# The depthwise convolution of a two-block transformer kernel: from VectorE and GpSimd to VectorE alone

## The chip, the cores and the metric

The kernel runs on one core of a Trainium2 chip. The metric is the device time of one execution in microseconds (us), as the median over several runs. The engines are named as in the profile: PE is TensorE (PEld its weight loads), DVE is VectorE, ACT is ScalarE, POOL is GpSimd, and SP issues the weight stream's DMAs.

## What is computed

The reference runs two transformer blocks on 256 tokens of width 2048, in fp32. In the first block, the input projection feeds three mixers: a gated linear recurrence (sections a_f, a_q, a_i, a_g), a dilated attention (b_q, b_k, b_v) and a convolution module. The change touches only that module:

```python
def conv_module(a, gate, conv_w, conv_b, ln_g, ln_b):
    u = a * jax.nn.sigmoid(gate)
    y = lax.conv_general_dilated(u, conv_w[:, None, :], window_strides=(1,),
                                 padding=((C_KERNEL - 1, 0),),
                                 dimension_numbers=('NWC', 'WIO', 'NWC'),
                                 feature_group_count=C_WIDTH) + conv_b
    return jax.nn.silu(layer_norm(y, ln_g, ln_b))
```

It has 768 channels and 31 taps. Channels lie on partitions, so the module has 6 tiles of 128 channels x 256 tokens, and one tap of one tile is one multiply-add of 128x256 elements: 6 x 31 = 186 steps, each adding to what the step before left in the same tile.

## The kernel before

Every matrix product is made from fp32 weights split in two parts. The weights come as a stream of 1 MB blocks through four buffers (`raw`), in an order that is written out by hand (`SECTIONS`). For each block b, ScalarE makes the high part (`split_high`, line 530), DVE makes the low part as the difference (`split_low`, line 1685), and PE multiplies: first the high part with both parts of the activations (32 matmuls, line 1020, "high pass"), then the low part (16 matmuls, line 1029, "low pass"). There are two pairs of part buffers. ScalarE may start block b+2 once PE has begun the low pass of block b, DVE may start its split of b+2 once block b is done, and a `raw` buffer is free for the next load once DVE's split has read it. Each engine works through its own instruction list in order.

Around the change the order is:

- The start section makes the modulated activations and the two branches of the convolution module, and DVE multiplies them into `upad` (line 1792), six tiles with 30 zero columns ahead of each.
- The 16 blocks of a_f and a_q follow, one product each. DVE runs a loop of 16 rounds over them: one `split_low` and six steps of the convolution on tiles 0 to 2 (lines 1804 and 1807), three chains side by side, 93 steps in all.
- GpSimd does tiles 3 to 5 meanwhile (lines 460 and 465). It has no multiply-add here, so for each tap it scales the three tiles into a scratch tile `ctap` and adds them to `cy`: 93 scalings of 256 columns and 30 adds of 768 columns.
- DVE then scales `fP` and `kk`, 16 instructions (lines 1817 and 1818).
- The level stage runs over 43 blocks (a_i, b_v, b_k, b_q, a_g, and nine of gate). PE, ScalarE and DVE each go block by block; from the fifth block on each block has one of 36 "levels" of the recurrence beside it: DVE prepares operands (lines 1838 and 1839), advances two running products (lines 1846 and 1848), PE makes 8 small products (line 1207), DVE reads them (line 1867). The first 14 blocks (a_i and b_v) go in pairs: PE runs the high pass of two blocks (64 matmuls), then the low pass of both (32), and DVE makes both splits together. The four blocks before level 0 are the lead (`LAG`).
- At level 19 PE waits for the whole convolution and sums it for the layer norm.

The wait for GpSimd's steps is `pe.wait_ge(conv_side, CONV_SIDE)`, the one for DVE's is `pe.wait_ge(conv_tap, CONV_DVE * C_TAPS)`. A step waits on DVE's own counter `conv_tap` until the step before it in its chain has been written.

Of the kernel before, what the change touches and what calls it, by code (L numbers as in the profile page):

```python
# [7 lines left out]
ALU = mybir.AluOpType  # L8
# [6 lines left out]
S = 256  # L15
# [6 lines left out]
A_HEADS, B_HEADS, B_SLOTS = 8, 12, 4  # L22
C_TILES, C_TAPS = 6, 31
EARLY = 2
CONV_DVE = 3
CONV_SIDE = (C_TILES - CONV_DVE) * C_TAPS + C_TAPS - 1
FF1, FF2 = 8192 // P, 5632 // P
QUARTER = 4
UP2 = FF2 // QUARTER
# [122 lines left out]
def two_blocks_kernel(nc, stream, x_t, ctx_t, vec_d, const_d, lvl_mask_d, ident_d, rel_bias, c_rows, scratch, x_keep, out_t):  # L152
    with ExitStack() as ctx:
# [3 lines left out]
        def sem(name):  # L157
            return ctx.enter_context(nc.semaphore(name))
# [47 lines left out]
        def v(name, i=0, n=1):  # L206
            return vec[:, VEC[name] + i:VEC[name] + i + n]
# [18 lines left out]
        bv = region(33024, 2, 768)  # L226
        squares = region(18432, 6, S)
        upad = region(19968, 6, 30 + S)
        ctap = region(18432, 3, S)
        cg = region(22016, 6, S)  # L230
        cy = yc = region(28672, 6, S)
        yb = region(30208, 2, S)
# [88 lines left out]
        sq_part, x_ready, hf_part, hh_part, h_part = (sem(n) for n in ("sq_part", "x_ready", "hf_part", "hh_part", "h_part"))  # L321
        dve_step, act_step = sem("dve_step"), sem("act_step")
        brow_mm, brow_ready, brow_out, bias_in = sem("brow_mm"), sem("brow_ready"), sem("brow_out"), sem("bias_in")
        conv_tap, conv_side, mean_mm, conv_cent, yc_in, conv_done = (
            sem(n) for n in ("conv_tap", "conv_side", "mean_mm", "conv_cent", "yc_in", "conv_done"))
        lvl_prep, lvl_mm, lvl_read, o_mm, o_copied, ya_ready = (
            sem(n) for n in ("lvl_prep", "lvl_mm", "lvl_read", "o_mm", "o_copied", "ya_ready"))
        qk_mm, log_ready, exp_ready, dg_ready = sem("qk_mm"), sem("log_ready"), sem("exp_ready"), sem("dg_ready")
# [46 lines left out]
        def conv_tap_of(t, tap):  # L375

            return v("conv_w", t * C_TAPS + tap)
# [63 lines left out]
        @block.gpsimd  # L441
        def _(pool):
            pool.memset(eps, EPS).then_inc(eps_set, 1)
            pool.memset(cpad, 0.0).then_inc(fills, 1)
            pool.memset(ones[:, :], 1.0).then_inc(fills, 1)
            pool.memset(head_sum[:, :], 0.0).then_inc(fills, 1)
            pool.wait_ge(fills, 3)
            pool.memset(head_sum[:, 7:8], 1.0).then_inc(fills, 1)

            pool.wait_ge(brow_ready, 1)  # L450
            pool.memset(upad[:, :, 0:30], 0.0).then_inc(pads_set, 1)
            pool.wait_ge(pads_set, 1)
            pool.wait_ge(ca_read, 2)
            n = 0
            for tap in range(C_TAPS):
                if tap:
                    pool.wait_ge(conv_side, n)
                for t in range(CONV_DVE, C_TILES):
                    dst = ctap[:, t - CONV_DVE, :] if tap else cy[:, t, :]
                    pool.tensor_scalar(dst, upad[:, t, tap:tap + S], conv_tap_of(t, tap), None if tap else v("conv_b", t),  # L460
                                       ALU.mult, *(() if tap else (ALU.add,))).then_inc(conv_side, 1)
                    n += 1
                if tap:
                    pool.wait_ge(conv_side, n)
                    pool.tensor_tensor(cy[:, CONV_DVE:, :], cy[:, CONV_DVE:, :], ctap, ALU.add).then_inc(conv_side, 1)
                    n += 1
            assert n == CONV_SIDE


        @block.scalar  # L470
# [527 lines left out]
        def _(pe):  # L998
# [231 lines left out]
            for n in range(BESIDE_LEVELS):  # L1230
                s = n - LAG
                part, i = LATE[n]
                if part in ("a_i", "b_v"):
                    if i % 2 == 0:
                        rest = gemm_tokens(gb(part, i), opH, 2, later=True)
                    else:
                        rest()
                else:
                    gemm_T(gb(part, i), opH)
                if s % 9 == 0 and 0 < s <= 36:  # L1240
                    outputs(s // 9 - 1)
                if s == 19:

                    pe.wait_ge(conv_tap, CONV_DVE * C_TAPS)
                    pe.wait_ge(conv_side, CONV_SIDE)
                    for t in range(C_TILES):
                        ins = pe.matmul(M[2][:, S:512], ones[:, :], cy[:, t, :], start=(t == 0), stop=(t == C_TILES - 1))
                    ins.then_inc(mean_mm, 1)
                if s == 22:
                    norm(squares, C_TILES)  # L1250
                if 0 <= s < 36:
                    level(s)
                if s in (36, 37):
                    for h in range(6) if s == 36 else range(6, 8):
                        pe.wait_ge(o_sq, h // 2 + 1)
                        ins = pe.matmul(M[0][0:8, 0:S], head_sum[:, 7 - h:15 - h], fP[:, h, :], start=(h == 0), stop=(h == 7))
                    if s == 37:
                        norms[0] += 1
                        ins.then_inc(ms_ready, 1)
# [385 lines left out]
        def _(dve):  # L1645
# [147 lines left out]
                ins.then_inc(ca_read, 1)  # L1793
            split_low(KT + 1)

            taps = 0
            for i in range(16):
                split_low(gb("a_f") + i + 2)
                if i == 0:
                    dve.wait_ge(ca_read, 3)  # L1800
                for _ in range(min(6, C_TAPS * CONV_DVE - taps)):
                    t, j = taps % CONV_DVE, taps // CONV_DVE
                    if j == 0:
                        ins = dve.tensor_scalar(cy[:, t, :], upad[:, t, 0:S], conv_tap_of(t, 0), v("conv_b", t), ALU.mult, ALU.add)
                    else:
                        dve.wait_ge(conv_tap, taps - CONV_DVE + 1)
                        ins = dve.scalar_tensor_tensor(cy[:, t, :], upad[:, t, j:j + S], conv_tap_of(t, j), cy[:, t, :],  # L1807
                                                       ALU.mult, ALU.add)
                    ins.then_inc(conv_tap, 1)
                    taps += 1  # L1810
            assert taps == C_TAPS * CONV_DVE

            for i in range(8):
                was_read(dve, gb("a_f", i))
# [10 lines left out]

            for n in range(LAG):
                split_late(n)

            for s in range(36):
                quarter, L = s // 9, s % 9  # L1830
                hs = slice(2 * quarter, 2 * quarter + 2)
                f_, q_, k_ = fP[:, hs, :], qq[:, hs, :], kk[:, hs, :]
                if L == 0:
                    dve.memset(suf, 1.0).then_inc(lvl_prep, 1)
                    dve.wait_ge(lvl_prep, s + 1)
                else:
                    dve.wait_ge(lvl_mm, s)
                    dve.tensor_tensor(qs, q_, f_, ALU.mult)
                    dve.tensor_tensor(ks, k_, suf, ALU.mult).then_inc(lvl_prep, 1)
                    dve.wait_ge(lvl_prep, s + 1)  # L1840
                    if L < 8:
                        w = 1 << (L - 1)
                        fv_ = f_.rearrange("p h (b two w) -> p (h b) two w", two=2, w=w)
                        sv_ = suf.rearrange("p h (b two w) -> p (h b) two w", two=2, w=w)
                        nb = 2 * S // (2 * w)
                        step(dve.tensor_tensor(sv_[:, :, 0, :], sv_[:, :, 0, :],
                                               fv_[:, :, 1, w - 1:w].to_broadcast([P, nb, w]), ALU.mult))
                        step(dve.tensor_tensor(fv_[:, :, 1, :], fv_[:, :, 1, :],
                                               fv_[:, :, 0, w - 1:w].to_broadcast([P, nb, w]), ALU.mult))

                if s == 20:
                    dve.wait_ge(mean_mm, 1)
                    step(dve.tensor_scalar(rstd[:, S:512], M[2][:, S:512], 1.0 / (C_TILES * P), None, ALU.mult))
                    dve.tensor_tensor(cy, cy, over_tiles(rstd[:, S:512], C_TILES), ALU.subtract).then_inc(conv_cent, 1)
                if s == 23:
                    inverted()
                    dve.wait_ge(conv_cent, 1)
                    dve.tensor_tensor(cy, cy, over_tiles(rstd[:, 0:S], C_TILES), ALU.mult).then_inc(yc_in, 1)
                split_late(s + LAG)
                dve.wait_ge(lvl_mm, s + 1)  # L1860
                if s % 9 == 0 and s:
                    dve.wait_ge(o_mm, quarter)
                bank4 = M[s % 2][:, :].rearrange("p (a b) -> p a b", a=4)
                if L == 0:
                    last = dve.tensor_tensor(attn, bank4, over_tiles(ident[:, :], 4), ALU.mult)
                elif L < 8:
                    last = dve.copy_predicated(attn, lvl_mask[:, L:L + 1, :].to_broadcast([P, 4, P]), bank4)
                else:
                    last = dve.tensor_copy(attx, bank4[:, 0:2, :])
                last.then_inc(lvl_read, 1)  # L1870
                dve.wait_ge(lvl_read, s + 1)

            split_late(36 + LAG)
            split_late(37 + LAG)
            inverted()
# [531 lines left out]
```

## Time and profile before

| | |
|---|---|
| median of 3 runs | 3377.06 us (3375.75 to 3380.68) |
| the profiled execution | 3368.44 us, its span 3366.6 us |
| PE, DVE, ACT, POOL busy | 96%, 68%, 40%, 6% of the span |
| mean granted PE clock | 0.98 of 2.4 GHz |
| a_f and a_q blocks | about 155 to 254 us |
| level stage: paired blocks, then single ones | about 254 to 356 us, then to about 560 us |

The profiled execution is 8.6 us under the median of the runs. Times in the trace count from the start of the span. A timeline row gives its start, its length, the engine, the line, the operation, output and inputs, the number of instructions merged in it, and in brackets how long the engine sat idle before it and what ended that.

### The profile page before, as it was taken

What the parts mean: (1) busy time and instruction counts of PE and PEld (TensorE: products, weight loads), DVE (VectorE), ACT (ScalarE), POOL (GpSimd) and SP (SyncE); (2) the same over time, 40 slices, a digit from 0 to 9 for tenths busy, and PEclk for the clock granted to TensorE, in tenths of its full rate; (3) what the DMA queues carried; (4) which work ended last, traced back from release to release, by engine and by line L of the source; (5) the groups of instructions that cost most, each with busy time, mean ns of one, the idle gap of its engine ahead of it and who ended that gap; (6) DMA issues with size and microseconds to landing.
All of it is one profiled execution on the core that took longest, in us unless ns stands there. A gap on an engine that the chain in (4) does not pass through costs nothing.

```text
span 3366.6 us, 59486 instructions
## 1 busy us (share of the span) xinstructions
PE 3236.8 (96%) x26148; PEld 3131.8 (93%) x26148; DVE 2279.4 (68%) x2532; ACT 1332.6 (40%) x1455; POOL 214.6 (6%) x133
## 2 busy tenths in 40 slices
PE   7898999899998999999999999999998999999998
PEld 6898999799998999999998899989888999999998
DVE  2498765578877778888956756644566666666664
ACT  2332344433434433333355233421355444343444
POOL 0199400000000000000000000000000000000000
PEclk9999999999999999999999999999999999999999
DMA  9854434388885687767744754354333575655643
GB/s 349 328 183 153 171 139 146 113 306 331 321 313 192 247 325 257 272 240 286 287 168 154 287 222 185 121 208 159 117 126 124 176 251 184 217 214 188 238 168 120
DMA packets 106430, 722.87 MB, mean 215 GB/s; under 512 B 11676, under 2 KB 15388, under 8 KB 27196
## 3 DMA queue, kind: packets, MB, share of 16 engines
q1 hardware_dynamic: 100368, 703.64, 56.9%
q10 hardware_dynamic: 5804, 15.43, 1.5%
q8 instruction: 207, 3.39, 0.4%
q14 instruction: 51, 0.42, 0.0%
HBM read 712.40 MB, written 6.55 MB: 214 GB/s over the span
## 4 chain that ended last, share of the span: by engine, by line
PE 88%; DVE 7%; DMA 2%; ACT 1%; issue 1%; ACTq 0%; DVEq 0%
PE gemm L1020 49%; PE gemm L1029 25%; DVE sb_arena L1807 2%; DVE sb_parts L1685 2%; PE mix L1108 2%; DMA sb_raw<-stream 2%; PE mix L1020 1%; PE gemm L1143 1%; PE mix L1207 1%; PE mix L1468 1%; DMA sb_arena<-x_t 1%; ACT sb_parts L530 1%; DVE sb_arena L1731 1%; PE mix L1029 1%; PE gemm L1537 1%
## 5 line engine op out<-in xcount | busy, mean ns | idle before, releaser
L530 ACT ACTIVATE sb_parts<-sb_raw 128x2048 fp32r<-128x2048 f32 (+2 forms) x499 | 913.6, 1833 | 1683.4 <-PE gemm L1029 1387.0
L1685 DVE TENSOR_TENSOR sb_parts<-sb_raw,sb_parts 128x2048 fp32r<-128x2048 f32 (+2 forms) x499 | 1096.3, 2198 | 400.1 <-ACT sb_parts L530 220.3
L1020 PE MATMUL gemm<-op_h,sb_parts 128*128 128x256 f32 x7232 | 899.3, 283 | 0.5 <-DVE sb_arena L1792 0.5
L1020 PEld LDWEIGHTS gemm<-op_h,sb_parts 128*128 128x128 f32 x7232 | 875.6, 189 | 1.5 <-issue 0.9
L1029 PE MATMUL gemm<-op_h,sb_parts 128*128 128x256 f32 x3616 | 466.8, 282 | 5.9 <-DVE sb_parts L1685 5.9
L1029 PEld LDWEIGHTS gemm<-op_h,sb_parts 128*128 128x128 f32 x3616 | 444.8, 188 | 7.3 <-DVE sb_parts L1685 7.3
L1020 PE MATMUL gemm<-op_up,sb_parts 128*128 128x256 f32 x3456 | 438.7, 284 | 11.4 <-DVE op_up L2246 11.4
L1020 PEld LDWEIGHTS gemm<-op_up,sb_parts 128*128 128x128 f32 x3456 | 422.8, 189 | 13.7 <-DVE op_up L2246 12.2
L1029 PE MATMUL gemm<-op_up,sb_parts 128*128 128x256 f32 x1728 | 228.2, 284 | 0.0
L1666 DVE CUSTOM_DVE_ANT_0 sb_raw<-sb_raw,sb_arena,sb_vec 128x2048 f32<-128x2048 f32 x96 | 224.3, 2348 | 1.1
L1029 PEld LDWEIGHTS gemm<-op_up,sb_parts 128*128 128x128 f32 x1728 | 216.2, 190 | 0.0
L1020 PE MATMUL gemm<-op_hw,sb_parts 128*128 128x512 f32 (+1 forms) x992 | 185.0, 344 | 0.0
L1020 PEld LDWEIGHTS gemm<-op_hw,sb_parts 128*128 128x128 f32 x992 | 156.8, 189 | 23.6
L1658 DVE CUSTOM_DVE_ANT_0 sb_raw<-sb_raw,sb_arena,sb_vec 128x2048 f32<-128x2048 f32 x64 | 149.8, 2346 | 0.0
L2237 DVE SCALAR_TENSOR_TENSOR sb_arena<-gemm,sb_vec,sb_arena 128x255 f32<-128x255 f32 x88 | 42.5, 483 | 150.0 <-ACT sb_arena L971 150.0
L460 POOL TENSOR_SCALAR sb_arena<-sb_arena,sb_vec 128x256 f32<-128x256 f32 x93 | 127.6, 1385 | 114.2 <-DVE sb_arena L1792 111.3
L1020 PE MATMUL gemm<-sb_parts,op_hw 128*128 128x256 f32 x1024 | 125.7, 286 | 0.9 <-ACT sb_parts L530 0.9
L1020 PEld LDWEIGHTS gemm<-sb_parts,op_hw 128*128 128x128 f32 x1024 | 124.3, 191 | 2.1 <-ACT sb_parts L530 1.1
L1974 DVE TENSOR_TENSOR sb_arena<-gemm,sb_arena 128x256 f32<-128x256 f32 x80 | 33.9, 424 | 102.8 <-PE gemm L1029 102.8
L1029 PE MATMUL gemm<-op_hw,sb_parts 128*128 128x512 f32 (+1 forms) x496 | 94.9, 344 | 0.0
L1108 PE MATMUL mix<-sb_arena,sb_ones 128*128 128x256 f32 x256 | 74.0, 419 | 19.1 <-ACT sb_arena L498 19.1
L1029 PEld LDWEIGHTS gemm<-op_hw,sb_parts 128*128 128x128 f32 x496 | 78.9, 189 | 11.9
(341 smaller groups left out, 3483.7 us busy)
## 6 DMA issues: line engine op xcount, KB each, us to landing
sb_raw<-stream SPq DMA_DIRECT2D x611, 1024.0 KB, 5.0
sb_raw<-stream SPq DMA_DIRECT2D x64, 704.0 KB, 4.1
sb_raw<-stream SPq DMA_DIRECT2D x16, 768.0 KB, 7.8
sb_arena<-c_rows ACTq DMA_DIRECT2D x3, 1024.0 KB, 8.1
bias_rows<-sb_arena ACTq DMA_DIRECT2D x1, 2304.0 KB
sb_arena<-x_t ACTq DMA_DIRECT2D x4, 512.0 KB, 17.9
sb_arena<-ctx_t SPq DMA_DIRECT2D x1, 2048.0 KB, 10.8
x_keep<-sb_arena ACTq DMA_DIRECT2D x1, 2048.0 KB, 6.3
```

Source lines behind the costliest of these rows:

```text
L460: pool.tensor_scalar(dst, upad[:, t, tap:tap + S], conv_tap_of(t, tap), None if tap else v("conv_b", t), ALU.mult, *(() if tap else (ALU.a ...
L530: act.activation(parts[:, b % 2, 0, 0:kt, :], raw[:, slot, 0:kt, :], ACT.Copy).then_inc(hi_ready, 1)
L1020: ins = pe.matmul(out, l, r, start=(opens and i == 0 and x is xh), stop=False, skip_group_check=True)
L1029: ins = pe.matmul(out, l, r, start=False, stop=(i == len(terms) - 1), skip_group_check=True)
L1108: ins = pe.matmul(M[1][:, 0:S], ones[:, :], src[:, k, :], start=(k == 0), stop=(k == KT - 1))
L1143: ins = pe.matmul(out[:, i * S:(i + 1) * S], w, opH[:, p, k, :], start=(k == i == part == p == 0), stop=(k == KT - 1 and part == 1), skip_ ...
L1658: dve.tensor_tensor_reduce(w, w, c1_row, 1.0, v("b_ada", a), ALU.mult, ALU.add, mod1[:, a:a + 1])\
L1666: dve.tensor_tensor_reduce(w, w, c2_row, 1.0, v("b_mod", a), ALU.mult, ALU.add, mod2[:, 0, a:a + 1])\
L1685: dve.tensor_tensor(parts[:, b % 2, 1, 0:kt, :], raw[:, slot, 0:kt, :], parts[:, b % 2, 0, 0:kt, :].bitcast(F32), ALU.subtract).then_inc(t ...
L1807: ins = dve.scalar_tensor_tensor(cy[:, t, :], upad[:, t, j:j + S], conv_tap_of(t, j), cy[:, t, :], ALU.mult, ALU.add)
L1974: dve.tensor_tensor(t, bank(b0 + j)[:, 0:S], t, ALU.add).then_inc(bank_read[BANK[b0 + j]], 1)
L2237: step(dve.scalar_tensor_tensor(y[:, 1:S], src[:, 0:S - 1], w0, y[:, 1:S], ALU.mult, ALU.add))
```

## The change

All 186 steps run on DVE, in six chains, one for each tile, tap after tap. They are spread: eight steps after each of the 16 splits of the a_f and a_q loop (128), five after each of the four lead steps (20), three in each level until none is left (38, levels 0 to 12). GpSimd keeps only the memset of the padding columns; `ctap` and `conv_side` go. DVE's wait on its own counter `ca_read` moves ahead of the first split of the loop. PE's wait at level 19 is for the one counter.

```diff
-CONV_DVE = 3
-CONV_SIDE = (C_TILES - CONV_DVE) * C_TAPS + C_TAPS - 1
+CONV_STEPS = C_TILES * C_TAPS
...
             pool.memset(upad[:, :, 0:30], 0.0).then_inc(pads_set, 1)
-            pool.wait_ge(pads_set, 1)
-            pool.wait_ge(ca_read, 2)
-            n = 0
-            for tap in range(C_TAPS):
-                if tap:
-                    pool.wait_ge(conv_side, n)
-                for t in range(CONV_DVE, C_TILES):
-                    dst = ctap[:, t - CONV_DVE, :] if tap else cy[:, t, :]
-                    pool.tensor_scalar(dst, upad[:, t, tap:tap + S], conv_tap_of(t, tap), None if tap else v("conv_b", t),
-                                       ALU.mult, *(() if tap else (ALU.add,))).then_inc(conv_side, 1)
-                    n += 1
-                if tap:
-                    pool.wait_ge(conv_side, n)
-                    pool.tensor_tensor(cy[:, CONV_DVE:, :], cy[:, CONV_DVE:, :], ctap, ALU.add).then_inc(conv_side, 1)
-                    n += 1
...
-                    pe.wait_ge(conv_tap, CONV_DVE * C_TAPS)
-                    pe.wait_ge(conv_side, CONV_SIDE)
+                    pe.wait_ge(conv_tap, CONV_STEPS)
...
-            taps = 0
-            for i in range(16):
-                split_low(gb("a_f") + i + 2)
-                if i == 0:
-                    dve.wait_ge(ca_read, 3)
-                for _ in range(min(6, C_TAPS * CONV_DVE - taps)):
-                    t, j = taps % CONV_DVE, taps // CONV_DVE
+            taps = [0]
+
+            def conv_taps(n):
+                for _ in range(min(n, CONV_STEPS - taps[0])):
+                    j, t = divmod(taps[0], C_TILES)
                     if j == 0:
                         ins = dve.tensor_scalar(cy[:, t, :], upad[:, t, 0:S], conv_tap_of(t, 0), v("conv_b", t), ALU.mult, ALU.add)
                     else:
-                        dve.wait_ge(conv_tap, taps - CONV_DVE + 1)
+                        dve.wait_ge(conv_tap, taps[0] - C_TILES + 1)
                         ins = dve.scalar_tensor_tensor(cy[:, t, :], upad[:, t, j:j + S], conv_tap_of(t, j), cy[:, t, :],
                                                        ALU.mult, ALU.add)
                     ins.then_inc(conv_tap, 1)
-                    taps += 1
-            assert taps == C_TAPS * CONV_DVE
+                    taps[0] += 1
+
+            dve.wait_ge(ca_read, 3)
+            for i in range(16):
+                split_low(gb("a_f") + i + 2)
+                conv_taps(8)
...
             for n in range(LAG):
                 split_late(n)
+                conv_taps(5)
...
                 split_late(s + LAG)
+                conv_taps(3)
                 dve.wait_ge(lvl_mm, s + 1)
```

## Rows read from the trace of the kernel before

**Rows 1.** The page, part 1: busy time, share of the span and instructions.

```profile
PE 3236.8 (96%) x26148; PEld 3131.8 (93%) x26148; DVE 2279.4 (68%) x2532; ACT 1332.6 (40%) x1455; POOL 214.6 (6%) x133
```

**Rows 2.** Busy time of each engine by stretch, with the mean granted clock.

```profile
core 0: us, PE busy (x) PEld busy (x) DVE busy (x) ACT busy (x) POOL busy (x), PEclk, DMA share, GB/s
...
265.60:288.40 22.80, 18.39 (x128) 18.24 (x129) 17.38 (x21) 8.03 (x5) 22.16 (x16) 0.85 0.38 139
288.40:356.40 68.00, 67.54 (x571) 67.10 (x570) 60.30 (x52) 22.29 (x18) 66.37 (x36) 1.00 0.42 156
```

**Rows 3.** Timeline of PE, the a_f and a_q blocks (matmuls only).

```profile
160.75 3.96 PE L1020 MATMUL gemm<-op_h,sb_parts 128*128 128x256 f32 x32
164.55 2.06 PE L1029 MATMUL gemm<-op_h,sb_parts 128*128 128x256 f32 x16
166.45 3.96 PE L1020 MATMUL gemm<-op_h,sb_parts 128*128 128x256 f32 x32
...
217.76 2.16 PE L1029 MATMUL gemm<-op_h,sb_parts 128*128 128x256 f32 x16 [0.86 <-DVE sb_parts L1685]
```

**Rows 4.** Timeline of PE, the first pairs of the level stage.

```profile
254.59 7.83 PE L1020 MATMUL gemm<-sb_parts,op_h 128*128 128x256 f32 x64 [0.49 <-ACT sb_parts L530]
265.69 5.55 PE L1029 MATMUL gemm<-sb_parts,op_h 128*128 128x256 f32 x32 [3.27 <-DVE sb_parts L1685]
271.07 7.76 PE L1020 MATMUL gemm<-sb_parts,op_h 128*128 128x256 f32 x64
283.16 5.47 PE L1029 MATMUL gemm<-sb_parts,op_h 128*128 128x256 f32 x32 [4.32 <-DVE sb_parts L1685]
288.46 7.75 PE L1020 MATMUL gemm<-sb_parts,op_h 128*128 128x256 f32 x64
296.06 1.05 PE L1207 MATMUL mix<-sb_arena 128*128 128x128 f32 x8
296.86 4.04 PE L1029 MATMUL gemm<-sb_parts,op_h 128*128 128x256 f32 x32
```

**Rows 5.** Timeline of DVE, one round of the a_f loop.

```profile
174.43 2.28 DVE L1685 TENSOR_TENSOR sb_parts<-sb_raw,sb_parts 128x2048 fp32r<-128x2048 f32 x1
176.63 4.71 DVE L1807 SCALAR_TENSOR_TENSOR sb_arena<-sb_arena,sb_vec 128x256 f32<-128x256 f32 x6
181.27 2.28 DVE L1685 TENSOR_TENSOR sb_parts<-sb_raw,sb_parts 128x2048 fp32r<-128x2048 f32 x1
```

**Rows 6.** Line 1807 (chained steps): ns min/median/max, first and last start.

```profile
L1807 DVE SCALAR_TENSOR_TENSOR sb_arena<-sb_arena,sb_vec x90: 470/694/2070, 166.3 to 268.1; 128x256 f32<-128x256 f32 x90
```

**Rows 7.** Timeline of POOL beside that round.

```profile
171.67 3.01 POOL L460 TENSOR_SCALAR sb_arena<-sb_arena,sb_vec 128x256 f32<-128x256 f32 x3
174.77 3.65 POOL L465 TENSOR_TENSOR sb_arena<-sb_arena 128x768 f32<-128x768 f32 x1
```

**Rows 8.** Lines 1817 and 1818 (16 scales): ns min/median/max, first and last start.

```profile
L1817 DVE TENSOR_SCALAR sb_arena<-sb_arena,sb_small x8: 480/558/1999, 268.4 to 277.4; 128x256 f32<-128x256 f32 x8
...
L1818 DVE TENSOR_SCALAR sb_arena<-sb_arena,sb_small x8: 348/530/531, 268.9 to 277.8; 128x256 f32<-128x256 f32 x8
```

**Rows 9.** Timeline of DVE in a later stage, GpSimd idle.

```profile
2573.40 0.48 DVE L1731 SCALAR_TENSOR_TENSOR sb_arena<-sb_arena,sb_small,sb_rstd 128x256 f32<-128x256 f32 x1
2573.79 0.48 DVE L1737 SCALAR_TENSOR_TENSOR op_h<-sb_arena,sb_mod,op_h 128x256 fp32r<-128x256 f32 x1
```

**Rows 10.** Timeline of DVE, one level of the single-block stage, GpSimd idle.

```profile
384.61 0.73 DVE L1867 COPY_PREDICATED sb_arena<-sb_lvl_mask,mix 128x512 f32<-128x512 uint8 x1
385.38 0.69 DVE L1838 TENSOR_TENSOR sb_arena<-sb_arena 128x512 f32<-128x512 f32 x1
...
386.71 0.43 DVE L1846 TENSOR_TENSOR sb_arena<-sb_arena 128x256 f32<-128x256 f32 x1
...
389.00 2.29 DVE L1685 TENSOR_TENSOR sb_parts<-sb_raw,sb_parts 128x2048 fp32r<-128x2048 f32 x1 [1.40 <-ACT sb_parts L530]
```

**Rows 11.** Timeline of ACT: the load that came late.

```profile
191.60 1.92 ACT L530 ACTIVATE sb_parts<-sb_raw 128x2048 fp32r<-128x2048 f32 x1 [7.13 <-DMA sb_raw<-stream]
```

More of the change, by code:

```diff
@@ L228, in two_blocks_kernel @@
         upad = region(19968, 6, 30 + S)
-        ctap = region(18432, 3, S)
         cg = region(22016, 6, S)
@@ L323, in two_blocks_kernel @@
         brow_mm, brow_ready, brow_out, bias_in = sem("brow_mm"), sem("brow_ready"), sem("brow_out"), sem("bias_in")
-        conv_tap, conv_side, mean_mm, conv_cent, yc_in, conv_done = (
-            sem(n) for n in ("conv_tap", "conv_side", "mean_mm", "conv_cent", "yc_in", "conv_done"))
+        conv_tap, mean_mm, conv_cent, yc_in, conv_done = (
+            sem(n) for n in ("conv_tap", "mean_mm", "conv_cent", "yc_in", "conv_done"))
         lvl_prep, lvl_mm, lvl_read, o_mm, o_copied, ya_ready = (
@@ L451, in _ @@
             pool.memset(upad[:, :, 0:30], 0.0).then_inc(pads_set, 1)
-            pool.wait_ge(pads_set, 1)
-            pool.wait_ge(ca_read, 2)
-            n = 0
-            for tap in range(C_TAPS):
-                if tap:
-                    pool.wait_ge(conv_side, n)
-                for t in range(CONV_DVE, C_TILES):
-                    dst = ctap[:, t - CONV_DVE, :] if tap else cy[:, t, :]
-                    pool.tensor_scalar(dst, upad[:, t, tap:tap + S], conv_tap_of(t, tap), None if tap else v("conv_b", t),
-                                       ALU.mult, *(() if tap else (ALU.add,))).then_inc(conv_side, 1)
-                    n += 1
-                if tap:
-                    pool.wait_ge(conv_side, n)
-                    pool.tensor_tensor(cy[:, CONV_DVE:, :], cy[:, CONV_DVE:, :], ctap, ALU.add).then_inc(conv_side, 1)
-                    n += 1
-            assert n == CONV_SIDE
         @block.scalar
@@ L1871, in _ @@
                 dve.wait_ge(lvl_read, s + 1)
+            assert taps[0] == CONV_STEPS
             split_late(36 + LAG)
```

## The prediction

> **What bounds the kernel now.** I read the page first. PE is busy 96% of the span [rows 1]. So the engine that loses the conv (GpSimd, 6%) and the one that takes it over (DVE, 68%) matter only where PE waits for DVE. The busy shares by stretch then say where that is [rows 2]: from 265.6 to 288.4 us PE works 18.39 of 22.80 us at a mean granted clock of 0.85, and from 288.4 to 356.4 us 67.54 of 68.00 at 1.00.
>
> PE's own timeline gives the size. A block of the a_f and a_q sections takes 166.45 - 160.75 = 5.70 us when nothing is late, 1.90 of it the low pass [rows 3]. DVE's round beside it, one low split and six taps, takes 181.27 - 174.43 = 6.84 us [rows 5]. At first PE lives on a lead, because DVE's split is due only 3.8 us into a block; once the lead is used up each low pass waits for DVE, 0.86 us in the row at 217.76 us [rows 3], seven such rows in all. After block 16 the waits go on: 3.27 us before the low pass of the first pair and 4.32 us before that of the second [rows 4]. After each of these two the low pass of 32 matmuls takes 5.38 and 5.30 us instead of 3.80 (2 x 1.90), and the mean granted clock of that stretch is 0.85, so part of it ran at 1.2 instead of 2.4 GHz.
>
> **Why DVE's round is that long.** The split takes 176.63 - 174.43 = 2.20 us, six taps 4.64 us, 0.773 each [rows 5]. The 90 taps range from 0.47 to 2.07 us with a median of 0.69 [rows 6], for one and the same size. In each round GpSimd runs three scalings and an add of 768 columns; the add at 174.77 us takes 3.65 us and so ends some 1.8 us into DVE's taps [rows 7]. The 16 scales that DVE does next, also beside GpSimd, show the same spread, 0.35 to 2.00 us [rows 8]. With GpSimd idle, the same instruction on the same size (SCALAR_TENSOR_TENSOR, 256 columns, all in SBUF) starts every 0.39 to 0.40 us (2573.40 and 2573.79, and 20 more such rows up to 2581.71, 0.396 on the mean) [rows 9]. I take 0.396 us for a tap after the change.
>
> The Trainium skill (SBUF — State Buffer, "SBUF: two separate sides") says that a DVE operation with two SBUF inputs and a GpSimd operation that reads SBUF hold a shared port pair exclusively, and the loser blocks for the whole instruction. The add row agrees; beside the scalings of about 1.0 us [rows 7] the median tap is only about 0.2 us longer than the shortest, which is less than that rule would give. With GpSimd idle both come to the same.
>
> **The change, part by part.**
>
> 1. *GpSimd's 93 scalings and 30 adds go.* They are not on the chain (their result is waited for at level 19, about 420 us; they end at 373 us). What they cost is DVE's delay, counted below.
>
> 2. *Eight taps a round instead of six, 16 rounds.* DVE: 2.20 + 8 x 0.396 = 5.37 us, under PE's 5.70. So PE sets the pace. From 160.75 us, where block 2 starts, 15 blocks end at 160.75 + 15 x 5.70 = 246.2 us; before, they ended at 254.59 - 0.49 = 254.1 us [rows 3, 4]. Gain 7.9 us. DVE's round is then held by ScalarE's high part, which ends about 0.2 us after the block, and its last round ends at 246.4 + 5.4 = 251.8 us. The wait for `ca_read` now stands ahead of the first split; it is DVE's own earlier instruction, nothing but that split is behind it, I bound it by 0 and the 2.2 us of a split, and take 0: it is hidden by ScalarE's high part.
>
> 3. *The 16 scales behind the stage* took 9.9 us beside GpSimd. They are not edited, but the two slowest lose 1.5 us each. I take 0.48 us each, 7.6 us, though 0.35 may do [rows 8]: DVE is at 259.4 us.
>
> 4. *Five taps after each of the four lead steps* add 2.0 us each. PE: first pair high pass from 246.7 us (0.49 behind ScalarE, as before), low from 254.3; its split is ready at 248.6. No wait, 3.27 + 1.58 us gone. Low ends at 258.1. DVE: five taps to 261.4, two splits (2 x 2.20) to 265.8. PE: high pass of the second pair 258.5 (again behind ScalarE, which the stall hid before: minus 0.47) to 266.1, then low. The split is 0.3 us early: 4.32 + 1.50 us gone. Low ends at 269.9. DVE: ten taps to 269.8, splits from 270.2 to 274.6, five taps and the memset to 277.2. PE's third pair: high pass 270.4 (minus 0.30) to 278.0, and level 0 finds its operands ready. Gain of this stretch 3.27 + 1.58 + 4.32 + 1.50 - 0.77 = 9.9 us.
>
> 5. *Three taps in each of levels 0 to 12* (38 in all: 186 - 128 - 20) add 1.2 us each. A level costs DVE 389.00 - 384.61 - 1.40 = 3.0 us [rows 10]. In the pair stage, two levels: 2 x 3.0 + 2 x 2.2 + 6 x 0.396 = 12.8 us against PE's 11.4 + 2 x 0.80 = 13.0 [rows 4]. The order inside matters more: from the end of a low pass DVE does two splits, three taps, the bank read (0.77) and the next operands (1.33) [rows 10], ready about 8.0 us later with the 0.3 us that ScalarE takes; PE wants them after a level and a high pass, 0.8 + 7.6 = 8.4 us. Now, beside GpSimd, PE is idle only some 0.5 us of this stage (68.00 - 67.54, [rows 2]); I let that go too. In the single-block stage DVE idles 1.40 us a level [rows 10]; three taps leave 0.2.
>
> 6. *From level 13 on* the instruction streams are the same, and the conv is finished (level 12) well ahead of its use at level 19. What is due after is relative to PE, so the gain is kept.
>
> Sum: 7.9 + 9.9 + 0.5 = 18.3 us. The profiled execution took 3368.44 us (span 3366.6 and 1.84 around it); after, 3350.1. The median of the runs shown is 8.6 us above that execution, so I put the change on it: 3377.06 - 18.3 = 3358.8, say 3359 us. Bounds: PE's waits and slow matmuls between 206 and 356 us, with the 0.77 us that stay, are 7.9 + 10.7 + 0.5 = 19 us, so the gain ends near there, 21 with what I don't see. From the other side a tap costs 0.48 if nothing overlaps, 0.773 if GpSimd was never the cause.
>
> **Rivals.**
>
> A. *Taps don't overlap: 0.48 us each, the record's own length [rows 9].* Then a round is 2.28 + 8 x 0.48 = 6.12 us, over 5.70. PE's lead covers all 16 rounds, but DVE leaves the stage at 259.1 us, has the scales and five taps done at 269.2, the two splits at 273.8, where PE wanted them at 267.2: 6.6 us and 1.5 of low clock; 1 us before the first pair. Gain 18.3 - 9.1 = 9 us, 3368. Against it: starts 0.396 apart [rows 9]. The Trainium skill (VectorE: DVE Perf Modes, "The DRAIN you can't avoid") would have it so: the next operation does not start until the pipe is empty. The trace's overlapping records speak against that here. The same outcome, a gain of 7 to 14 us, comes if the thin margins of parts 4 and 5 (0.3 and 0.4 us) are missed, each miss costing itself and up to 1.5 us of clock. Chance of both together 0.17.
>
> B. *Slower: the tap's price is its own, not GpSimd's.* If a tap stays at 0.773, a round is 8.4 us: the last ends near 294 us, against 268.4 now, 26 us later; ten of the extra taps before the levels add 8 us, the pair stage 5 x (4.6 - 0.7) = 20 us, three single levels 2 us: 56 us, 3433. Where it turns: at 0.58 a round is as long as now (2.2 + 8 x 0.58 = 6.84), and the taps between stage and levels and those in the pair stage make it some 7 us slower; at 0.50 the same count leaves a gain of 7; so about 0.54. For it: the taps now cost 0.77 on the mean. Against it: the same instruction in [rows 9], and the 0.47 of the shortest taps [rows 6]. Chance 0.05, all prices above 0.54 together.
>
> C. *No change: PE goes faster but the weights don't come.* At 191.60 us ScalarE waited 7.13 us for a load [rows 11], while the stage's one store was still going out. If the stream held PE at its old pace, nothing would be won: 3377. Against it: PE took its blocks at the full 5.70 us up to about 206 us, this late load among them, and the stream kept up. A late load more likely costs 1 to 3 us. Chance of within 0.2%: 0.07.
>
> D. *More than 22 us*, by something that I don't see: 0.03.
>
> **How the numbers follow.** The forecast (3355 to 3362) has 0.68, A 0.17, B 0.05, C 0.07, D 0.03. 0.2% is 6.8 us, about what a measurement of this kernel tells from no change. A still counts as faster: 0.68 + 0.17 + 0.03 = 0.88. The range takes in A: 3353 to 3369.
>
> **What would show it.** Right: PE's blocks start 5.70 us apart up to about 246 us and the second pair's low pass starts without a wait; the 180 chained taps last 0.47 to 0.48 us each, none 2 us; DVE's split has a short idle before it, put down to ScalarE, in each round; the 1.2 GHz stretches at 265.9 and 282.9 us are gone; from level 13 the trace is the old one, 18 us earlier. Wrong: taps over 0.5 us, a PE wait on the DVE split behind the 16 scales, levels whose operands PE waits for.

## The result, and the profile after

The changed kernel took 3360.18 us (median of 5 runs, 3347.63 to 3365.33) against 3379.46 us for the kernel before (5 runs, 3375.75 to 3382.06): a ratio of 0.9948, 95% interval 0.993 to 0.9966. Faster by 19.3 us; 18.3 were forecast, 3359 us as the time.

PE's timeline answers [rows 3] and [rows 4]. The blocks come every 166.68 - 160.98 = 5.70 us, up to the last; of the two long waits nothing is left, and 0.4 to 0.5 us of waiting for ScalarE stand ahead of each of the first three pairs:

```profile
160.98 3.96 PE L1002 MATMUL gemm<-op_h,sb_parts 128*128 128x256 f32 x32
...
166.68 3.96 PE L1002 MATMUL gemm<-op_h,sb_parts 128*128 128x256 f32 x32
...
247.07 7.83 PE L1002 MATMUL gemm<-sb_parts,op_h 128*128 128x256 f32 x64 [0.49 <-ACT sb_parts L512]
254.74 3.96 PE L1011 MATMUL gemm<-sb_parts,op_h 128*128 128x256 f32 x32
259.10 7.84 PE L1002 MATMUL gemm<-sb_parts,op_h 128*128 128x256 f32 x64 [0.40 <-ACT sb_parts L512]
266.77 3.95 PE L1011 MATMUL gemm<-sb_parts,op_h 128*128 128x256 f32 x32
271.12 7.83 PE L1002 MATMUL gemm<-sb_parts,op_h 128*128 128x256 f32 x64 [0.40 <-ACT sb_parts L512]
278.79 1.06 PE L1189 MATMUL mix<-sb_arena 128*128 128x128 f32 x8
```

DVE's timeline answers [rows 5] and [rows 8]. Eight steps take 3.25 us, 0.40 each, and the split that follows has waited 0.24 us for ScalarE. The 16 scales, now lines 1802 and 1803, start 0.29 us apart on the mean:

```profile
172.81 2.29 DVE L1666 TENSOR_TENSOR sb_parts<-sb_raw,sb_parts 128x2048 fp32r<-128x2048 f32 x1 [0.23 <-ACT sb_parts L512]
175.01 3.25 DVE L1788 SCALAR_TENSOR_TENSOR sb_arena<-sb_arena,sb_vec 128x256 f32<-128x256 f32 x8
178.50 2.29 DVE L1666 TENSOR_TENSOR sb_parts<-sb_raw,sb_parts 128x2048 fp32r<-128x2048 f32 x1 [0.24 <-ACT sb_parts L512]
...
252.23 0.41 DVE L1802 TENSOR_SCALAR sb_arena<-sb_arena,sb_small 128x256 f32<-128x256 f32 x1
252.55 0.35 DVE L1803 TENSOR_SCALAR sb_arena<-sb_arena,sb_small 128x256 f32<-128x256 f32 x1
252.81 0.41 DVE L1802 TENSOR_SCALAR sb_arena<-sb_arena,sb_small 128x256 f32<-128x256 f32 x1
...
257.04 2.07 DVE L1788 SCALAR_TENSOR_TENSOR sb_arena<-sb_arena,sb_vec 128x256 f32<-128x256 f32 x5
259.03 4.49 DVE L1666 TENSOR_TENSOR sb_parts<-sb_raw,sb_parts 128x2048 fp32r<-128x2048 f32 x2
```

The 180 chained steps all last the same (ns min/median/max; [rows 6] had 470/694/2070):

```profile
L1788 DVE SCALAR_TENSOR_TENSOR sb_arena<-sb_arena,sb_vec x180: 470/478/486, 165.6 to 360.9; 128x256 f32<-128x256 f32 x180
```

The busy shares of the stretch that was at a mean clock of 0.85 in [rows 2] (PE, PEld, DVE, ACT, POOL, then the clock): PE works 22.40 of 22.80 us, all at 2.4 GHz.

```profile
265.60:288.40 22.80, 22.40 (x190) 22.23 (x189) 17.53 (x24) 8.47 (x6) 0.00 (x0) 1.00 0.39 148
```

A measure that leaves out what happens elsewhere is the distance from PE's first a_f block to the first single block of the level stage (block 14), read from PE's timeline. It is 356.36 - 154.97 = 201.4 us before and 338.23 - 155.21 = 183.0 us after: 18.4 us less.

But the two profiled spans differ by 8.3 us only (3366.6 and 3358.3). DVE's splits, numbered from 0 at the start of the kernel, show where the rest went. Number 150 starts 18.9 us earlier than before (1056.7 against 1075.6 us), number 270 only 11.9 (1756.9 against 1768.8), number 300 only 9.4. Between 1100 and 1650 us PE is busy all the time at a granted clock of 1.00; it simply does fewer matmuls in the same 550 us. Of before, then of after:

```profile
core 0: us, PE busy (x), PEclk, DMA share, GB/s
1100.00:1650.00 550.00, 550.00 (x4637) 1.00 0.75 272
```

```profile
core 0: us, PE busy (x), PEclk, DMA share, GB/s
1100.00:1650.00 550.00, 550.00 (x4586) 1.00 0.75 272
```

That is 118.6 ns from matmul to matmul before and 119.9 after. This distance is called the pitch below, and a part of a trace at 119.9 a slow stretch. Whether it came with the change had to be tested.

### The profile page after: what moved, and what is told of

The parts are those of the page before. It is cut to its first block, busy times and chain, and to the rows that moved or that the text cites. A ratio compares the mean times of both kernels' runs of the same rounds, so it can differ in the third digit from the quotient of the medians.

```text
span 3358.3 us, 59453 instructions
## 1 busy us (share of the span) xinstructions
PE 3243.2 (97%) x26148; PEld 3137.8 (93%) x26148; DVE 2261.3 (67%) x2625; ACT 1332.7 (40%) x1455; POOL 1.7 (0%) x10
## 4 chain that ended last, share of the span: by engine, by line
PE 92%; DVE 4%; DMA 2%; ACT 1%; issue 1%; ACTq 0%; DVEq 0%
PE gemm L1002 51%; PE gemm L1011 25%; PE mix L1090 2%; DMA sb_raw<-stream 2%; PE mix L1002 1%; PE gemm L1125 1%; PE mix L1189 1%; PE mix L1449 1%; ACT sb_parts L512 1%; DMA sb_arena<-x_t 1%; DVE sb_parts L1666 1%; DVE sb_arena L1712 1%; PE mix L1011 1%; PE gemm L1518 1%; PE gemm L1525 1%
## 5 line engine op out<-in xcount | busy, mean ns | idle before, releaser
L1975 DVE TENSOR_TENSOR sb_arena<-sb_arena 128x256 f32<-128x256 f32 x64 | 27.1, 424 | 75.1 <-ACT sb_arena L756 73.6
```

## The experiments

In the table, "between" is the distance from the first a_f block to block 14 in the one profiled execution of each kernel. The second trace of the kernel before comes from a single execution of 3381.74 us. Ratios are against the kernel before, run on the same chip in the same job.

| kernel | median us | ratio, 95% interval | between, us |
|---|---|---|---|
| before (first trace; again) | 3379.46 | 1 | 201.4; 201.5 |
| changed | 3360.18 | 0.9948 (0.993 to 0.9966) | 183.0 |
| changed, again | 3356.11 | 0.9946 (0.9925 to 0.9966) | 183.1 |
| changed, third | 3353.70 | 0.9939 (0.992 to 0.9958) | 183.1 |
| before, GpSimd's half left out | 3358.81 | 0.9944 (0.9922 to 0.9965) | 182.9 |
| changed, one chain | 3367.21 | 0.9967 (0.9953 to 0.9981) | 190.3 |
| changed, GpSimd beside | 3408.85 | 1.0095 (1.0067 to 1.0124) | 236.6 |
| changed, GpSimd scalings only | 3365.12 | 0.997 (0.9957 to 0.9983) | 192.9 |
| changed, GpSimd adds only | 3394.05 | 1.0049 (1.0031 to 1.0066) | 221.3 |
| changed, twelve a round | 3370.09 | 0.9982 (0.9969 to 0.9994) | 197.1 |
| changed, split ahead of the norm | 3351.62 | 0.9924 (0.9906 to 0.9942) | 183.1 |
| the same, again | 3351.89 | 0.9936 (0.9917 to 0.9956) | 183.2 |

**The changed kernel again**, with no edit.

> The changed kernel again, nothing altered. In its first trace the block after the single-block boundary (block 14 of the level stage) starts 18.1 us earlier than before, but PE's matmuls of the up and down stretches (1114 to 1672 us) follow one another by 120.0 ns where the kernel before had 118.6, which gives some 9 us back. Theory P (the two pitches are a state that an execution falls into): the part up to 338 us repeats within 0.5 us (block 14 starts at 338), while the stretches at 120 ns lie elsewhere or are gone, and the end moves with them, by up to 10 us. Rival Q (the slower pitch comes with the change): the same stretches at 120 ns again, and the same end.

The distance repeated within 0.1 us and the slow stretch was gone; the span was 3348.7 us, 9.6 less than in the first trace of the same kernel, some 7 of them by the pitch:

```profile
core 0: us, PE busy (x), PEclk, DMA share, GB/s
1100.00:1650.00 550.00, 550.00 (x4637) 1.00 0.75 276
```

**GpSimd's half left out of the kernel before.** DVE's part is as it was: three chains, six steps a round.

```diff
-CONV_SIDE = (C_TILES - CONV_DVE) * C_TAPS + C_TAPS - 1
+CONV_SIDE = 1
...
-            for tap in range(C_TAPS):
...
+            pool.memset(cy[:, CONV_DVE:, :], 0.0).then_inc(conv_side, 1)
```

> The kernel before, with GpSimd's half of the convolution left out: tiles 3 to 5 are set to zero by one memset, DVE still does its 93 steps, six a round. Theory (GpSimd's SBUF traffic lengthens DVE's steps): a step follows the next by 0.396 us instead of 0.773, DVE's round is 2.2 + 6 x 0.396 = 4.6 us, PE sets the pace with 5.70, no wait before the low passes of the first two pairs, block 14 of the level stage starts at 338 us as in the changed kernel (356.4 before), the end about 18 us under the kernel before. Rival (a step costs 0.77 by itself, or the gain comes from six chains instead of three): the round stays at 6.8 us and the time within 2 us of the kernel before.

The same six steps as in [rows 5] take 2.46 us instead of 4.71, DVE is idle 1.03 us a round, and PE waits for it nowhere. The distance is 182.9 us. So the whole gain of 18.4 us had been the price of GpSimd's work beside DVE, and nothing of them is due to six chains or to the spreading, which only keep the price of the added steps at nothing. (This kernel computes only three of the six tiles; it measures time alone.)

```profile
174.79 2.46 DVE L1794 SCALAR_TENSOR_TENSOR sb_arena<-sb_arena,sb_vec 128x256 f32<-128x256 f32 x6
178.28 2.29 DVE L1672 TENSOR_TENSOR sb_parts<-sb_raw,sb_parts 128x2048 fp32r<-128x2048 f32 x1 [1.03 <-ACT sb_parts L517]
```

**One chain.** Tile after tile, each step waiting for the one ahead.

```diff
-                    j, t = divmod(taps[0], C_TILES)
+                    t, j = divmod(taps[0], C_TAPS)
...
-                        dve.wait_ge(conv_tap, taps[0] - C_TILES + 1)
+                        dve.wait_ge(conv_tap, taps[0])
```

> The changed kernel, but the 186 steps run tile after tile, so that each waits for the one ahead of it to be written. Theory (six chains let the steps overlap; a dependent DVE operation starts about 0.03 us after the end of the one ahead, so 0.51 us apart): round 2.2 + 8 x 0.51 = 6.3 us, over 5.70, DVE leaves the a_q stage near 262 us instead of 252, PE waits some 3 us before the low pass of the first pair and some 3 us before that of the second, with low-clock stretches behind; block 14 starts near 347 instead of 338, the time 7 to 11 us over the changed kernel. Rival (the waits are free, the order doesn't matter): same as the changed kernel within 2 us.

Eight dependent steps take 176.18 - 172.13 = 4.05 us, 0.506 each, as expected, and PE waits 1.98 us before the low pass of the first pair and 3.58 us before that of the second. The distance grows by 7.2 us, the median by 11 us over the changed kernel run beside it.

```profile
172.13 4.13 DVE L1788 SCALAR_TENSOR_TENSOR sb_arena<-sb_arena,sb_vec 128x256 f32<-128x256 f32 x8
176.18 2.28 DVE L1666 TENSOR_TENSOR sb_parts<-sb_raw,sb_parts 128x2048 fp32r<-128x2048 f32 x1
```

```profile
259.18 4.04 PE L1011 MATMUL gemm<-sb_parts,op_h 128*128 128x256 f32 x32 [1.98 <-DVE sb_parts L1666]
...
275.09 5.19 PE L1011 MATMUL gemm<-sb_parts,op_h 128*128 128x256 f32 x29 [3.58 <-DVE sb_parts L1666]
```

**GpSimd beside.** The changed kernel with GpSimd's old loop kept, its sums going to a scratch tile.

```diff
+                    dst = ctap[:, t - CONV_DVE, :] if tap else cside[:, t - CONV_DVE, :]
...
+                    pool.tensor_tensor(cside, cside, ctap, ALU.add).then_inc(conv_side, 1)
```

> The changed kernel, with GpSimd also doing its old 93 scalings and 30 adds, into scratch that nobody reads; PE waits for them at level 19 as before. Theory (contention): a step costs 0.77 us again, the round is about 8.4 us, block 14 starts near 410 us, and the time is 40 to 75 us over the changed kernel and well over the kernel before. Rival (GpSimd beside DVE costs little when DVE has six chains): within 10 us of the changed kernel.

The median is 53 us over the changed kernel and 31 over the kernel before, so the sign of the change hangs on GpSimd being idle. A round takes 183.47 - 175.61 = 7.86 us, some longer, less than the 8.4 expected; block 14 starts at 389 us, not 410.

```profile
175.61 2.28 DVE L1687 TENSOR_TENSOR sb_parts<-sb_raw,sb_parts 128x2048 fp32r<-128x2048 f32 x1
177.81 5.73 DVE L1809 SCALAR_TENSOR_TENSOR sb_arena<-sb_arena,sb_vec 128x256 f32<-128x256 f32 x8
183.47 2.28 DVE L1687 TENSOR_TENSOR sb_parts<-sb_raw,sb_parts 128x2048 fp32r<-128x2048 f32 x1
```

**Which of GpSimd's instructions.** The same kernel with the 93 scalings alone, and with the 30 adds alone. The main lines left out are shown; the scalings then follow one another without a wait, and so do the adds, which in the full loop lie some 7 us apart.

```diff
-                    pool.wait_ge(conv_side, n)
-                    pool.tensor_tensor(cside, cside, ctap, ALU.add).then_inc(conv_side, 1)
```

```diff
-                    pool.tensor_scalar(dst, upad[:, t, tap:tap + S], conv_tap_of(t, tap), None if tap else v("conv_b", t),
-                                       ALU.mult, *(() if tap else (ALU.add,))).then_inc(conv_side, 1)
```

> The changed kernel with GpSimd beside it doing 93 scalings of 256 columns into a scratch tile, and no adds. Theory (a scaling lengthens a DVE step by some 0.2 us every other time, the add by 1.6): steps 0.5 us apart on the mean, round about 6.3 us, the time 6 to 12 us over the changed kernel. Rival (a GpSimd instruction of any kind keeps a two-input DVE operation out for its whole length): steps at least 1 us apart while GpSimd runs, 40 us or more over the changed kernel.

> The changed kernel with GpSimd beside it doing 30 adds of 768 columns in scratch, and no scalings. Theory: each add (1.83 us, two inputs in SBUF) keeps one DVE step waiting for about 1.6 us, 30 x 1.6 = 48 us of DVE time at the start of the a_f stage; with PE's lead of 6 us and a few us of DVE idle taken off, 30 to 42 us over the changed kernel. Rival (the scalings are what costs, being three times as many): under 15 us over the changed kernel.

Beside the scalings, eight steps take 179.04 - 175.06 = 3.98 us, 0.50 each, the longest 0.70 us; the distance grows by 9.8 us. Beside the adds the steps are 1.96 us apart (15.68 for eight) and even the split takes 3.88 instead of 2.28; GpSimd's 30 adds (ns min/median/max) run one behind the other until 222 us, and one DVE step gets in between two of them. The distance grows by 38.2 us. Apart the two cost 48.0 us of distance, together (the kernel with both) 53.5, and the adds have most of it in both counts. How the 18.4 us of the kernel before divide between them was not measured. DVE timeline of the first kernel with its chained steps and GpSimd's scalings (ns min/median/max), then of the second (with the six unchained first steps, one input each, ahead), and GpSimd's line in the second:

```profile
175.06 4.06 DVE L1804 SCALAR_TENSOR_TENSOR sb_arena<-sb_arena,sb_vec 128x256 f32<-128x256 f32 x8
179.04 2.28 DVE L1682 TENSOR_TENSOR sb_parts<-sb_raw,sb_parts 128x2048 fp32r<-128x2048 f32 x1
```

```profile
L1804 DVE SCALAR_TENSOR_TENSOR sb_arena<-sb_arena,sb_vec x180: 469/479/704, 165.7 to 369.9; 128x256 f32<-128x256 f32 x180
```

```profile
L461 POOL TENSOR_SCALAR sb_arena<-sb_arena,sb_vec x93: 922/1035/4846, 154.2 to 288.3; 128x256 f32<-128x256 f32 x93
```

```profile
162.38 11.54 DVE L1800 TENSOR_SCALAR sb_arena<-sb_arena,sb_vec 128x256 f32<-128x256 f32 x6
...
181.61 15.75 DVE L1803 SCALAR_TENSOR_TENSOR sb_arena<-sb_arena,sb_vec 128x256 f32<-128x256 f32 x8
197.29 3.88 DVE L1681 TENSOR_TENSOR sb_parts<-sb_raw,sb_parts 128x2048 fp32r<-128x2048 f32 x1
```

```profile
L461 POOL TENSOR_TENSOR sb_arena<-sb_arena x30: 1812/1862/3775, 154.6 to 218.6; 128x768 f32<-128x768 f32 x30
```

**Twelve steps a round**, not spread.

```diff
-                conv_taps(8)
+                conv_taps(12)
```

> The changed kernel with the steps not spread: twelve after each split of the a_f and a_q loop, so all but six are done in it and none is left for the levels. Theory (DVE's round against PE's 5.70 decides): round 2.2 + 12 x 0.396 = 6.95 us, PE's lead of some 6 us lasts five or six rounds, then PE goes at DVE's pace, and the low pass of the first pair waits until about 268 us (254.7 in the changed kernel); block 14 starts at 351 to 354 us instead of 338, the time is 13 to 15 us over the changed kernel, only some 4 us under the kernel before. Rival (only the total of DVE's work counts, not where it lies): same as the changed kernel within 3 us.

DVE's round is 216.86 - 209.91 = 6.95 us. From 212 us on PE waits 0.9 to 1.0 us in each block, and 3.52 before the first pair's low pass, which starts at 267.99 us, at 268 as expected. 14.1 us of the 18.4 are gone: with the steps placed so, the removal of GpSimd's work would have bought 4.3 us of distance. The median is 7.1 us under the kernel before (3377.23 us in that job), where some 4 were expected.

```profile
209.91 2.29 DVE L1666 TENSOR_TENSOR sb_parts<-sb_raw,sb_parts 128x2048 fp32r<-128x2048 f32 x1
212.11 4.84 DVE L1788 SCALAR_TENSOR_TENSOR sb_arena<-sb_arena,sb_vec 128x256 f32<-128x256 f32 x12
216.86 2.29 DVE L1666 TENSOR_TENSOR sb_parts<-sb_raw,sb_parts 128x2048 fp32r<-128x2048 f32 x1
```

```profile
267.99 5.56 PE L1011 MATMUL gemm<-sb_parts,op_h 128*128 128x256 f32 x32 [3.52 <-DVE sb_parts L1666]
```

**One edit more: the low split ahead of the norm at level 23.**

```diff
-                if s == 23:
-                    inverted()
-                    dve.wait_ge(conv_cent, 1)
-                    dve.tensor_tensor(cy, cy, over_tiles(rstd[:, 0:S], C_TILES), ALU.mult).then_inc(yc_in, 1)
                 split_late(s + LAG)
                 conv_taps(3)
+                if s == 23:
+                    inverted()
+                    dve.wait_ge(conv_cent, 1)
+                    dve.tensor_tensor(cy, cy, over_tiles(rstd[:, 0:S], C_TILES), ALU.mult).then_inc(yc_in, 1)
```

> The changed kernel, with one more edit: at level 23 DVE makes the low split first and then waits for the layer norm's root and scales cy, instead of the other way round. In the changed kernel's trace PE waits 2.15 us before level 24 for DVE's operands (wait for the root 441 us, scale 1.7, split 2.2, read, operands), and in some executions a 1.2 GHz stretch follows (1.4 us). Theory: the split goes into the time in which DVE waits for the root, the wait before level 24 falls from 2.15 us to under 0.5, the end comes 2 to 3.5 us earlier; against the spread of runs (PE pitch of 118.7 or 120 ns) the median may not show it, the trace's PE row at level 24 must. Rival (ScalarE's root is late enough that the scale still holds the operands): PE still waits 1 to 2 us there and nothing is gained.

> The version with the low split ahead of the layer norm's scale at level 23, beside the changed kernel on one chip. Theory: 2 to 4 us under the changed kernel, by the wait that is gone before level 24 (2.15 us) and the low-clock stretch that may follow it. Rival (the lower median of its first run came from PE's pitch alone): no difference beyond 1 us.

PE's row of level 24, in the changed kernel and in this one (its second trace): the wait of 2.15 us is gone.

```profile
445.86 1.16 PE L1189 MATMUL mix<-sb_arena 128*128 128x128 f32 x8 [2.15 <-DVE sb_arena L1825]
```

```profile
441.43 1.16 PE L1189 MATMUL mix<-sb_arena 128*128 128x128 f32 x8
```

Its two medians, 3351.6 and 3351.9 us, are the lowest of the study. Beside the changed kernel on one chip it is 1.8 us lower (3351.89 against 3353.70), between the 2 to 4 us expected and the rival's 1 us, with runs of each spread over 14 us, so the medians don't prove a gain. Nor do the traces show that it is kept: counted from PE's first a_f block, DVE's split number 150 comes after 900.3 and 900.7 us in the two traces of this version, and after 901.5, 900.2 and 901.9 us in the three of the changed kernel. What is shown is that the wait is gone; whether the kernel is shorter for it stays open.

**The slow PE pitch: one more trace of the changed kernel and one of the kernel before.**

> The changed kernel once more, on the same chip as the version with the split ahead of the norm. Theory P: the place of the stretches with 120 ns between matmuls differs again from the first trace's (1035 to 1702 us), the stage up to block 14 doesn't (from PE's first a_f block to block 14: 183.0 us, as in both traces so far); median 3354 to 3361.

> The kernel before, one look, for its PE pitch. Theory P: stretches with 120 ns can come up in it too, in places other than those of its first trace (3% of its blocks there). Rival Q (the slower pitch comes with the change): 3% again, and the same blocks. The waits before block 14 repeat: 3.3 and 4.3 us before the low passes of the first two pairs.

Both had the slow stretch. The distance repeated in both (183.1 and 201.5 us), and in the second trace of the kernel before PE waited 3.27 and 4.26 us before the low passes of the first two pairs, as in the first. That trace now shows the 4586 matmuls that the changed kernel's first trace had:

```profile
core 0: us, PE busy (x), PEclk, DMA share, GB/s
1100.00:1650.00 550.00, 550.00 (x4586) 1.00 0.73 268
```

So the pitch is a state of an execution and doesn't come with the change. My guess that the stretch would lie elsewhere each time was wrong for the long one: in every trace that has it (changed, first and third; one chain; before, second) it lies in the up and down sections. It begins behind a wait of PE of 2.81 us (which ends at 1033.55 us in the changed kernel's first trace) and ends where PE, without a stop, does 32 products of another kind (from 1694.26 us there). But there are others, and they do differ from execution to execution. Between 2590 and 2680 us the changed kernel's third trace and one chain have 752 matmuls, the changed kernel's first two traces 761; between 3130 and 3270 us the third trace has 1169 and the first 1182. All at a granted clock of 1.00. What picks the state stays open.

## Why the prediction was right

*Steps 2 to 4, the a_f and a_q blocks and the lead.* Right in size and place. The forecast had the first pair's low pass at 254.3 us (254.7 measured), its second at 266.1 (266.8), the third pair's high pass at 270.4 (271.1), level 0 at 278.0 (278.8). PE's own start was 0.2 us later than before. The price of a step, taken from a later stage in which GpSimd was idle [rows 9], was the number that everything hung on: 0.396 us forecast, 0.396 to 0.40 measured, and the run without GpSimd's half ties the old 0.773 to GpSimd.

*Step 3, the 16 scales.* Too dear: 7.6 us forecast, 4.8 measured (252.2 to 257.0 us). With the scales done earlier, DVE's splits for the second pair end at 263.5 us, over 3 us ahead of PE's low pass, where 0.3 us had been counted. It changed nothing in the sum, in which DVE only had to be early enough.

*Step 5, three steps in a level.* Right: PE waits for DVE's operands once up to level 23, 0.24 us at 344 us, in the first level of the single-block stage.

*Step 6, the gain is kept.* Right for the work (18.9 us at split number 150), not for one execution: the pitch state can take back or give 7 us in the up and down stretch alone. The forecast knew nothing of it. It would also explain why the profiled execution of before stood 8.6 us under the median: it was one with almost no slow stretch. That is likely and not shown, since the other runs have no trace.

*The time itself.* The gain of 18.3 us is confirmed by the distance, 18.4 us. That the median came within 2 us of the forecast of 3359 us is in part luck: the changed kernel's three medians are 3360.2, 3356.1 and 3353.7 us, and the kernel before beside them 3379.5, 3377.5 and 3372.0.

*Rival A* was told apart by the one-chain run: where steps really don't overlap (0.506 us), the loss is 7.2 us of distance; it had been put at 9. The Trainium skill (VectorE: DVE Perf Modes, "The DRAIN you can't avoid") has the next operation start only when the pipe is empty, but adds in the same paragraph that one that is not held back starts earlier; the prediction took up the first half alone. The changed kernel's steps start 0.396 us apart with records of 0.478 us, which agrees with the second half; only dependent ones go at 0.506.

*Rival B* would have had the loss without GpSimd. The loss comes only with GpSimd beside, and is then 31 us over the kernel before, where 56 had been counted from 0.773 a step; in the round shown a step took (183.47 - 177.81) / 8 = 0.71 us. *Rival C* didn't come: ScalarE's late load was there again, 6.4 us, and PE didn't wait for it.

## What to carry over

An engine that takes work off another can cost more than it takes, if the two get into each other's way: price a step with the helper idle (a like instruction elsewhere in the trace does) before dividing the work. Then place the work where its owner has air, round by round, against the pace of the engine that bounds: 5.37 us of DVE's work beside PE's 5.70 was free, 6.95 gave back 14 of 18 us.

## What the runs showed of the hardware

- GpSimd and DVE, all operands in SBUF, fp32: a GpSimd add (two inputs, 128x768, 1.84 us alone) keeps DVE's two-input operation out until it ends; in a row of adds DVE gets one step in between, so a step of 0.40 us costs 1.96. A GpSimd scaling (one input, 0.92 us alone, about 1.03 beside DVE's steps) only makes a step 0.50 us on the mean: two steps start within one scaling, and the longer record of the two is 0.70 us instead of 0.48. The Trainium skill (SBUF — State Buffer, "SBUF: two separate sides") makes no such difference between the two: any GpSimd instruction that reads SBUF would hold the shared port pair for its whole length. The adds agree; the scalings don't.
- The other way round DVE's split (two inputs, 2.28 us) keeps both out: in the kernel with scalings only, the scaling that starts at 172.70 us beside a split lasts 3.16 us, while the split keeps its length; in the one with adds only, the add beside a split lasts up to 3.78 us.
- The six 128x256 scales of DVE (one input, the first steps of the six chains) also took 11.54 us beside the adds, 1.92 each, against 0.32 in the changed kernel.
- At a granted clock of 1.00, the same stream of 128x128 by 256 fp32 matmuls ran at 118.6 or at 119.9 ns from one to the next, and kept its pace for 650 us. Two executions of one program differ by some 7 us for that stretch alone.
